# The half-swap of a rotary embedding: by TensorE's product or by DMA

## What is computed

```python
def _rotate(x, inv_freq):
    ang = jnp.arange(s)[:, None] * inv_freq[None, :]
    cos, sin = jnp.cos(ang), jnp.sin(ang)
    x1, x2 = x[..., : d // 2], x[..., d // 2:]
    return jnp.concatenate([x1 * cos - x2 * sin, x1 * sin + x2 * cos], -1)
```

## Time and profile before

| | us |
|---|---|
| median of 3 runs | 3569.78 (3568.07 to 3572.08) |
| the profiled execution, its time | 3564.92 |
| the profiled execution, its span | 3563.6 |
| PE busy | 3477.9 (98%) |
| DVE busy | 1881.9 (53%) |
| ACT busy | 1227.3 (34%) |
| POOL busy | 497.8 (14%) |
| mean granted TensorE clock | 0.987 |

### The profile page before, as it was taken

One profiled execution on the slowest core, in us unless ns is written; L12 is line 12 of the kernel. 1 busy time (PEld: TensorE's weight loads), 2 busy tenths in 40 slices (PEclk: granted clock), 3 DMA queues, 4 the chain that ended last, 5 costly groups with the idle time before them and its releaser, 6 DMA issues.

```text
span 3563.6 us, 41132 instructions
## 1 busy us (share of the span) xinstructions
PE 3477.9 (98%) x16780; PEld 2825.2 (79%) x16780; DVE 1881.9 (53%) x3243; ACT 1227.3 (34%) x1653; POOL 497.8 (14%) x438
## 2 busy tenths in 40 slices
PE   8999999999999999999999999989999999999999
PEld 5888877788888888866788887657888888888887
DVE  5545743654556455644752345786653345564333
ACT  3222472442225222563442234245432222342221
POOL 1010211210012000221210021112011110211111
PEclk9999999999999999999999999989999999999999
DMA  6444211133442344211232222101222222222221
GB/s 265 176 172 177 99 68 60 48 142 142 166 151 110 142 165 154 95 48 48 72 140 95 95 68 81 60 12 48 83 84 103 98 95 98 107 72 91 99 95 71
DMA packets 53039, 373.43 MB, mean 105 GB/s; under 512 B 5873, under 2 KB 6001, under 8 KB 10098
## 3 DMA queue, kind: packets, MB, share of 16 engines
q1 hardware_dynamic: 52850, 370.79, 28.7%
HBM read 368.67 MB, written 2.10 MB: 104 GB/s over the span
## 4 chain that ended last, share of the span: by engine, by line
PE 44%; DVE 4%; ACT 1%; issue 1%; POOL 0%; DVEq 0%; ACTq 0%; POOLq 0%
PE ps L1467 44%; DVE s_sm L2526 0%; PE ps L1487 0%; DVE s_bm L2528 0%; ACT s_wh L1802 0%; DVE s_hl L2111 0%; DVE s_wl L2118 0%; DVE s_tmp L2387 0%; DVE s_xr L2247 0%; DVE s_sm L2385 0%; DVE s_tmp L2545 0%; DVE s_sm L2365 0%; ACT s_tmp L1952 0%; DVE s_xx L2387 0%; DVE s_tmp L2237 0%
## 5 line engine op out<-in xcount | busy, mean ns | idle before, releaser
L1467 PE MATMUL ps<-s_hh,s_wh 128*128 128x512 f32 x2552 | 1012.7, 397 | 20.7 <-POOL s_hl L2680 13.1
L1467 PE MATMUL ps<-s_hh,s_wl 128*128 128x512 f32 x2552 | 999.6, 392 | 0.0
L1467 PE MATMUL ps<-s_hl,s_wh 128*128 128x512 f32 x2552 | 998.6, 391 | 0.0
L2118 DVE TENSOR_TENSOR s_wl<-s_stage,s_wh 128x2048 fp32r<-128x2048 f32 (+1 forms) x276 | 623.5, 2259 | 657.2 <-ACT s_wh L1802 657.0
L1802 ACT ACTIVATE s_wh<-s_stage 128x2048 fp32r<-128x2048 f32 (+1 forms) x276 | 519.1, 1881 | 585.4 <-PE ps L1467 432.8
L1467 PEld LDWEIGHTS ps<-s_hh,s_wh 128*128 128x128 f32 x2552 | 482.3, 189 | 138.8 <-issue 31.6
L1467 PEld LDWEIGHTS ps<-s_hh,s_wl 128*128 128x128 f32 x2552 | 482.0, 189 | 103.0
L1467 PE MATMUL ps<-s_ah,s_wh 128*128 128x512 f32 x1408 | 560.9, 398 | 0.1
L1467 PEld LDWEIGHTS ps<-s_hl,s_wh 128*128 128x128 f32 x2552 | 482.9, 189 | 98.0 <-issue 0.7
L1467 PE MATMUL ps<-s_ah,s_wl 128*128 128x512 f32 x1408 | 549.1, 390 | 0.0
L1467 PE MATMUL ps<-s_al,s_wh 128*128 128x512 f32 x1408 | 548.6, 390 | 0.0
(11 more groups left out here) (488 smaller groups left out, 3673.8 us busy)
## 6 DMA issues: line engine op xcount, KB each, us to landing
s_stage<-in_w_ada SPq DMA_DIRECT2D x64, 1024.0 KB, 4.8
s_stage<-in_ffn_w_gate SPq DMA_DIRECT2D x44, 1024.0 KB, 4.8
s_stage<-in_ffn_w_up SPq DMA_DIRECT2D x44, 1024.0 KB, 4.8
s_stage<-in_ffn_down SPq DMA_DIRECT2D x32, 1024.0 KB, 4.8
s_stage<-in_w_up SPq DMA_DIRECT2D x32, 1024.0 KB, 4.7
s_stage<-in_down_m SPq DMA_DIRECT2D x32, 1024.0 KB, 4.7
s_stage<-in_w_in SPq DMA_DIRECT2D x24, 1024.0 KB, 4.8
s_stage<-in_ffn_down SPq DMA_DIRECT2D x16, 768.0 KB, 4.3
```

Source lines behind the costliest of these rows:

```text
L1467: return pe.matmul(out, lhs, rhs, start=start, stop=stop, skip_group_check=True)
L2118: ins = dve.tensor_tensor(m.wl(ws)[:, a:z], m.STAGE[:, j % NS, a:z], m.wh(ws)[:, a:z].bitcast(F32), ALU.subtract)
```

## The change

`m_rope` loses its product on PE and its bank. A new step `m_swap` on SP copies the four blocks of 32 partitions of the tile, pairwise exchanged, into the temporary buffer with four DMAs on one semaphore. DVE multiplies that buffer with the sine table in place, and the sign that `perm1` held is now in the sine table. DVE and POOL wait for the fourth DMA instead of PE's product. In the generator the temporary buffer and `m_swap` come a tick earlier than `m_rope` came, and `m_rope` of a tile comes two ticks after its `m_swap`. The copy of tile 1 is put behind `m_rope` of tile 0. The parts of the diff below are, in order, the planner's generator, PE, DVE, POOL, SP and the constants.

```diff
         def roped(key, kind):
             for t in range(2):
+                q = self.tmp.take()
+                self.add("m_swap", l, key, t, q)
                 yield
-                b, q = self.banks.take(), self.tmp.take()
-                self.add("m_rope", l, key, t, kind, b, q)
-                self.banks.free(b, ("m.sin", l, key, t))
+                yield
+                self.add("m_rope", l, key, t, kind, q)
                 self.tmp.free(q, ("m.r", l, key, t))
...
-    def m_rope(l, key, t, kind, b, q):
-        e.wait_ge(("m.p", l, key, t), b.after)
-        mul(m.bank(b), m.perm1, m.t[key][:, t, :]).then_inc(*e.up("pe_rope", "m.turn", l, key, t))
...
-        e.wait_ge(("c1",), ("m.turn", l, key, t), q.after)
-        dve.tensor_tensor(m.tmp(q), m.bank(b), m.c1(kind + "_sin"), ALU.mult).then_inc(*e.up("dve_rope", "m.sin", l, key, t))
+        e.wait_ge(("c1",), ("m.turn", l, key, t, 3))
+        dve.tensor_tensor(m.tmp(q), m.tmp(q), m.c1(kind + "_sin"), ALU.mult).then_inc(*e.up("dve_rope", "m.sin", l, key, t))
...
-        e.wait_ge(("c1",), ("m.p", l, key, t), ("m.turn", l, key, t))
+        e.wait_ge(("c1",), ("m.p", l, key, t), ("m.turn", l, key, t, 3))
...
+    def m_swap(l, key, t, q):
+        e.wait_ge(("m.p", l, key, t), q.after)
+        for i in range(4):
+            a, b = 32 * i, 32 * (i ^ 1)
+            sp.dma_start(m.tmp(q)[a:a + 32, :], m.t[key][b:b + 32, t, :]).then_inc(
+                *e.up("turn_%s%d" % (key, t), "m.turn", l, key, t, i, by=16))
...
-    cc["perm1"] = perm(32, 64)
...
-        c1[name + "_sin"] = np.tile(np.sin(ang), (4, 1)).astype(f)
+        c1[name + "_sin"] = np.concatenate([-np.sin(ang), np.sin(ang)] * 2, 0).astype(f)
```

More of the change, by code:

```diff
@@ L1781, in tensor @@
         mm=mm, mm2=mm2, mmt=mmt, ada_row=ada_row, ada_turn=ada_turn, ada_col=ada_col, ada_sum=ada_sum, ln_mean=ln_mean, ln_var=ln_var,
-        ln_spread=ln_spread, rms_a=rms_a, rms_b=rms_b, root=root, m_rope=m_rope, sb_z=sb_z, sb_sum=sb_sum,
+        ln_spread=ln_spread, rms_a=rms_a, rms_b=rms_b, root=root, sb_z=sb_z, sb_sum=sb_sum,
         sb_av=sb_av, ret_s=ret_s, ret_av=ret_av,
@@ L2298, in glu, with m_rope @@
         dve.tensor_tensor(m.tmp(q), m.tmp(q), m.bank(b), ALU.mult).then_inc(*e.up("dve_ffn", "glu", pid))
-    def m_rope(l, key, t, kind, b, q):
+    def m_rope(l, key, t, kind, q):
         x = m.t[key][:, t, :]
-        e.wait_ge(("c1",), ("m.turn", l, key, t), q.after)
-        dve.tensor_tensor(m.tmp(q), m.bank(b), m.c1(kind + "_sin"), ALU.mult).then_inc(*e.up("dve_rope", "m.sin", l, key, t))
+        e.wait_ge(("c1",), ("m.turn", l, key, t, 3))
+        dve.tensor_tensor(m.tmp(q), m.tmp(q), m.c1(kind + "_sin"), ALU.mult).then_inc(*e.up("dve_rope", "m.sin", l, key, t))
         e.wait_ge(("m.sin", l, key, t), ("m.cos", l, key, t))
@@ L2821, in store @@
         e.wait_ge(("out", NT - 1))
-    run(plan, dict(begin=begin, wa_load=wa_load, x_load=x_load, issue=issue, begin_c1=begin_c1, c2_load=c2_load, pos_load=pos_load, x_begin=x_begin,
+    run(plan, dict(begin=begin, wa_load=wa_load, x_load=x_load, issue=issue, begin_c1=begin_c1, c2_load=c2_load, pos_load=pos_load, m_swap=m_swap, x_begin=x_begin,
                    store=store))
@@ L2891, in const @@
             self.later = ap
-        elif k == "perm1":
-            self.perm1 = ap
         elif k == "perm2":
```

## The result

The changed kernel takes 3584.71 us (median of 8 runs, 3575.25 to 3588.25) beside 3570.06 (8 runs, 3565.34 to 3572.08) for the kernel before: a ratio of 1.0043, 95% interval 1.0033 to 1.0052. It is slower by 15 us. The forecast was 3566.6, with a range up to 3579. The profiled execution took 3584.01, its span is 3582.7, the mean granted clock 0.981.

The account below looks back on a forecast made before the run. PE was taken as the bound, busy 3477.9 of 3563.6 us. Terms: -6.9 (products), -4.3 (bank waits), +6.0 (late dq/dk), +2.0 (clock) = -3.2 us on the median 3569.78, giving 3566.6; range 3556 to 3579.

Parts of the forecast that it names:

- Products of rq and rk: In rq/rk, removing eight swap products at 0.86 us each from a full PE saves 6.9 us.
- The rest at nothing: Everything else, including smaller constants and DVE's added work in rq/rk, covered by slack, was put at no cost.
- the waits for the banks: In rq/rk, PE's waits for banks `m_center` frees shrink: -4.3 us, between 0 (at worst nothing goes) and -9.7.
- I take a third of 8.0 ... and the 1.7 us in full: In rq/rk, 2.6 us of bank waits go, plus all 1.7 us of low clock after the second layer's wait.
- When the copies land: In dq/dk, 16 copies issue 0.45 us apart, 7.2 us in all; dq's tile 0 lands at about 618.2.
- DVE and POOL, 12.2 us: In dq/dk, six POOL products and eight DVE instructions run one after another, ending the last sum at 630.4.
- What that moves: The dilated attention's first masked score starts 3.0 us later a layer, +6.0 us in all, with PE idle for 7 us.
- Clock after that idle: After PE's idle before the dilated attention, a lower clock costs +1.0 us a layer, between 0 and 2.
- (b): Rival: in rq/rk the bank waits stay or move to another; +1.1 us, 3570.9. Chance 0.15.
- (c): Rival: SP's queue backs up on the dq/dk copies; slower, 3584 at 1.3 us an issue, 3598 at 2.0. Chance 0.14.
- (a): Rival: the rotation of dq and dk stays hidden; -11.2 to -9.8 us, 3558.6 to 3560. Chance 0.24.
- The signs: Forecast wrong if PE's idle before the first dilated score is under 3 or over 12 us, or rq/rk waits grow.

Follow-up runs that it names:

- rqrk: The kernel before with only the rotations of rq and rk by copy; dq and dk keep PE's product. 3569.94 us, ratio 0.9999.
- the base: The second profile of the unchanged kernel before (`again`), span 3566.6 us, against which the table of profiled executions counts gains and losses.
- ticks: The kernel before with one more yield ahead of each rotation, PE's swap product kept. 3572.09 us, ratio 1.0013.
- late_dma: `early_dma` with the rotations of rq and rk started after both chunks of rv. 3561.26 us, ratio 0.9982 to the kernel before.
- again: The kernel before, unchanged, run for a second profile. 3568.21 us, ratio 1.0000.
- dqdk: The kernel before with only the rotations of dq and dk by copy; rq and rk keep PE's product. 3588.55 us, ratio 1.0051.
- parity: The changed kernel with 16 banks taken and freed at once, restoring the ring's numbering. 3586.4 us, ratio 1.0053 to the kernel before.
- dqdk_at_once: `dqdk` with both tiles' copies issued at the generator's first step and rotations at the old ticks. 3585.48 us, ratio 1.0051 to the kernel before.
- center_pe: The kernel before with `m_center` written ahead of the tick that follows its product. 3576.9 us, ratio 1.0024.
- early_pe: The kernel before (PE's product) with dq and dk projected ahead of the two gate chunks. 3570.58 us, ratio 1.0000.
- early_dma: The changed kernel with dq and dk projected ahead of the two gate chunks. 3564.86 us, ratio 0.9986 to the kernel before.

## Why the prediction was wrong

**Which steps failed.** The table of profiled executions stands beside the sum of the prediction like this. Products of rq and rk with their bank waits were to give -11.2 us and gave -5.5. The stretch of dq and dk with its clock was to cost +8.0 and cost +11.0 (5.2 and 5.8). All the rest stood at nothing and cost +10.7: 3.3 between the mixers and 7.4 in the second block. The largest failure is thus "*The rest at nothing*". It gives a reason for the constants and for DVE's work, and none for the clock in the stretches that no edit touches; there PE ran longer at the lower level. Why it did was not found. The other two steps follow.

**Products of rq and rk, and the waits for the banks (-6.9 and -4.3).** Of -11.2 us the table has -5.5 (-5.4 and -0.1), and by the runs of `rqrk` nothing is left at the end. The price of a product, 0.86 us, was not tested by itself: of the 5.4 us, 3.4 are about what four products would give, but the base also has 3.4 us of low clock there that the kernel after has not, and `ticks` gains 5.0 with all products in place. The step that failed is "I take a third of 8.0 ... and the 1.7 us in full". The bound "at worst nothing goes" was too good: it named the mechanism, that the next score of stick-breaking finds the same DVE, and yet not its size. In the first layer the waits stay at 4.0 us. In the second they grow from 4.0 to 6.0, three takers now instead of two, which is one of the prediction's own signs of being wrong, and the low clock was not removed with them, it came elsewhere. The table by stretch of the kernel after has it twice:

```profile
1562.00:1566.00 4.00, 1.75 (x8) 0.61 (x8) 2.74 (x8) 3.64 (x5) 3.41 (x5) 0.87 0.00 0
...
1576.00:1580.00 4.00, 2.00 (x6) 0.88 (x7) 1.88 (x5) 1.07 (x3) 1.27 (x3) 0.83 0.00 0
```

PE is busy for half of each of them; in the kernel before it is busy for all of both, at 1.00. Together with the 2.0 us of longer waits that eats the 3.4 us of the four products. What delays DVE can be read in its timeline, between two `m_center`. The rotation is still there, and its sine product, beside POOL, takes more than twice as long as it did. Behind it, DVE stands for ACT in a step of stick-breaking that comes before the next `m_center`.

```profile
1553.92 1.65 DVE L2301 TENSOR_TENSOR s_tmp<-s_tmp,s_c 128x512 f32<-128x512 f32 x1
1555.60 1.67 DVE L2303 TENSOR_TENSOR s_rq<-s_rq,s_tmp 128x512 f32<-128x512 f32 x1
...
1561.29 0.42 DVE L2310 SCALAR_TENSOR_TENSOR s_nk<-ps,s_tmp 128x256 f32<-128x256 f32 x1 [1.49 <-ACT s_tmp L1918]
```

`late_dma`, which takes the rotation out of that stretch, gets the 5 us there.

The Trainium skill has the rule behind that duration in the page "SBUF — State Buffer" (section "SBUF: two separate sides"): DVE with two SBUF inputs and a GpSimd instruction that reads SBUF exclude each other for a whole instruction. The rows agree: 1.75 and 1.77 us beside POOL, 0.68 without. The prediction used it for dq and dk, and there it held; for rq and rk it put the growth down as covered. How much of the miss is the lock, and how much the units' chain itself, was not measured apart.

**When the copies land.** 0.45 us an issue was taken from the opening; it is 0.62 in the sets that waited for nothing, and all 16 took 11.1 us (609.33 to 620.46) where 7.2 were counted. The first tile was to be there at 618.2, which is 614.2 in the time of the kernel after (4.0 us ahead); it came at 615.5, 1.3 us late. In the second layer it came at 1672.8, 7.4 us after SP began with the copies (1665.45), against 6.2 in the first, and so 2.5 us late.

**DVE and POOL, 12.2 us.** Right. From the first landing to the end of the last sum it took 627.46 - 615.5 = 12.0 us, in the second layer 1684.71 - 1672.8 = 11.9. The last sum was foreseen at 630.4 and came at 627.46 + 4.0 = 631.4, in the time of the kernel before.

**What that moves (+3.0 a layer).** The first masked score starts 4.4 us late in the first layer (628.37 + 4.0 - 627.92) and 5.5 in the second, where 3.0 was forecast. The landing is 1.3 and 2.5 us of that miss. PE's score between the last sum and DVE is 0.4: it took 0.91 us (627.46 to 628.37) where I had 0.5, at the low clock. The shorter row of DVE and POOL gave 0.2 or 0.3 back. The idle of 7 us was 8.3 and 9.4. So the mechanism was the forecast's and the mis-sized term is the landing of the first tile.

**Clock after that idle (+1.0 a layer).** The clock stays low for 13.7 us in both layers, from 623 (0.52 over 623 to 637) and from 1678 (0.53 over 1678 to 1692), where the kernel before had 3.4 in the first layer and none in the second. Inside the attention this costs less than forecast, because PE often waits there: in the first layer it is 27.4 us from the first masked score to the output projection instead of 26.8. Two more stretches of 3.4 us follow in the first layer, at 657 and 718. The table by stretch of the kernel after shows the second of them; `again` has 1.00 at the same work.

```profile
716.00:723.00 7.00, 7.00 (x37) 6.16 (x37) 5.10 (x18) 2.56 (x3) 0.00 (x0) 0.76 0.41 151
```

PE is busy all through, so half of 3.4 us is lost each time, 3.4 in all; that is the +3.3 between the mixers. Whether the idle ahead of it is the reason is not shown: of the four kernels that have the long idle this stretch costs 3.3 and 3.2 (the kernel after and `dqdk`), but about 2 in `parity` and 1.5 in `dqdk_at_once`, and up to 1.7 in kernels without it.

**The rivals.** (b) was right about the waits, which stayed or moved, and not about the time: its +1.1 us (-6.9 for the products, +8.0 for dq/dk and the clock) leaves out 1.4 us at rq/rk, 3.0 of landing and clock at dq/dk, and the 10.7 in stretches that no edit touches. I had (b) and a mis-sized dq/dk as alternatives, where both can be true. (c) was wrong as a mechanism: s is 0.62, far from 1.07, although the time came out near its 3584. That is luck; a result that fits a rival's number is no evidence for its cause. One of its numbers was also added wrongly: at s = 2.0 its own formula gives a shift of 23.0 us a layer, a sum of +37 and 3607 us, not +28 and 3598. (a) fell with the wait of 8.3 us.

**The signs.** The idle before the first score, 8.3 and 9.4 us, lay inside the 3 to 12 that were to speak for the forecast, and the time was wrong all the same. The stretch of rq and rk was to be 4 to 8 us shorter in each layer; it was 5.4 in the first and 0.1 in the second.

**What stays open.** From 1704 on, no instruction was changed, and the changed kernels lose 1.5 (`center_pe`) to 7.7 us (`parity`) on the base there. The loss comes together with low clock in stretches where many small products stand among the weight products. This stretch of `again` and the same work in `rqrk` show it:

```profile
2320.00:2335.00 15.00, 12.49 (x68) 10.09 (x66) 9.88 (x28) 8.74 (x16) 0.00 (x0) 0.89 0.21 72
```

```profile
2315.00:2330.00 15.00, 12.49 (x44) 9.36 (x43) 9.14 (x24) 7.58 (x14) 0.00 (x0) 0.66 0.21 70
```

PE is busy as long, at a clock of 0.66 instead of 0.89, and from 2171 to 2332 `rqrk` loses 4.2 us on the base. The same loss is in `ticks` and `early_pe`, which copy nothing, and neither in the two profiles of the kernel before nor in `early_dma`, which copies all. It is thus not the DMAs; whether the shift in time is enough for it, or something else, was not tried. With the 3.3 between the mixers, whose cause is open too, it is 10.7 of the 16 us between the profiles. In `rqrk` the second block takes back (6.4 us) more than was gained until then (4.3).

## What to carry to other kernels

Before moving a step from a full engine to a slower path, look for the reader: the swap by DMA cost nothing that the times show where 26 us lay between the end of the rotation and its reader (`early_dma`), and 5 to 6 us a layer where it was the last thing before it. A wait that an instruction takes for a shared buffer belongs to whoever frees the buffer; removing the taker hands it to the next one. Where two parts of a change stand in different stretches, time each alone: their errors here had one sign. And when a sum of a few microseconds is forecast for a kernel of 3570, the stretches that the change leaves alone are a term too: here they moved by 10.7.

## What the runs showed of the hardware

- SP issues a copy of 64 KB from SBUF to SBUF every 0.62 us, and takes 0.43 for the load of 1 MB right before it (608.90 to 609.33): the smaller transfer is the dearer one for the queue.
- Four such copies behind a load of 1 MB are there 6.2 to 7.4 us after the first is issued. From issue to landing a copy took 4.4 to 5.5 us in the tile right behind the load (609 and 1665 us), 2.7 to 3.7 in the next one, and 1.9 to 2.0 in the last tile of the first layer (from 618 us).
- The sine product of 128x512 on DVE with both inputs in SBUF took 0.68 or 0.69 us alone and 1.65 to 1.77 beside POOL. POOL's cosine product took 1.27 us at 617.36, and 1.73 at 615.67, where DVE's product had begun 0.11 us before it.
- With an idle of 8.3 and 9.4 us the granted clock stood at the lower level for 13.7 us, though PE was at work again, with small products and waits, from 627.57 and 1684.82 (busy for 8.9 of the 14 us from 623, and for 6.6 of the 14 from 1678).
